# The order of VectorE's work around the start of a feed-forward: squares ahead of a low part, and a weight split behind a sum

## What is computed

```python
def second_block(x, mem, ...):
    for l in range(DEPTH):                       # DEPTH = 2
        ...
        y = memory_cross_attention(h, mem, xa_wq[l], xa_wkv[l], xa_wo[l], xa_mem_norm[l])
        x = x + rms_norm_2(y, g[3])
        h = rms_norm_2(x, g[4])
        y = sq_relu_mlp(h, mlp_w1[l], mlp_w2[l]) # jnp.square(relu(h @ w1)) @ w2, 1024 -> 4096 -> 1024
        x = x + rms_norm_2(y, g[5])
```

## Time and profile before

| | us |
|---|---|
| time, median of 3 runs (lowest, highest) | 1379.44 (1379.16, 1380.48) |
| the profiled execution | 1378.3 |
| its span, first to last instruction | 1376.5 |
| TensorE busy | 1361.0 (99%) |
| VectorE busy | 1013.3 (74%) |
| ScalarE busy | 743.4 (54%) |
| GpSimd busy | 98.0 (7%) |

### The profile page before, as it was taken

The page is one execution under the profiler, slowest core; times in us unless marked ns, Lnnn a source line. Parts: engine busy times, 40 slices in busy tenths (PEclk is TensorE's granted clock), DMA queues, the critical chain, the costliest instruction groups (busy, mean ns, idle before and its releaser), DMA issues.

```text
span 1376.5 us, 19424 instructions
## 1 busy us (share of the span) xinstructions
PE 1361.0 (99%) x7455; PEld 1135.9 (83%) x7455; DVE 1013.3 (74%) x1514; ACT 743.4 (54%) x1151; POOL 98.0 (7%) x104
## 2 busy tenths in 40 slices
PE   9999999999999999999999999999999999999998
PEld 6887888888888888888888778888888868888886
DVE  5666778777764777877787786886676876886665
ACT  4564555554545655654555666654445675654443
POOL 0000011000000000211111001120000000200000
PEclk9999999999999999999999999999999999999999
DMA  9844455555465435666655524368866523356552
GB/s 309 245 145 153 159 178 185 185 193 195 163 213 183 139 107 183 221 206 206 206 187 167 153 79 154 107 217 225 210 193 210 168 94 129 117 188 196 197 185 92
DMA packets 146578, 242.26 MB, mean 176 GB/s; under 512 B 4603, under 2 KB 91403, under 8 KB 146222
## 3 DMA queue, kind: packets, MB, share of 16 engines
q1 hardware_dynamic: 142498, 226.97, 50.5%
q0 software_dynamic: 3712, 13.77, 3.7%
q10 hardware_dynamic: 276, 0.27, 0.1%
HBM read 239.03 MB, written 1.97 MB: 175 GB/s over the span
## 4 chain that ended last, share of the span: by engine, by line
PE 92%; DVE 5%; ACT 2%; issue 1%; DMA 0%; POOL 0%; ACTq 0%; DVEq 0%
PE ps L1080 19%; PE ps L1046 16%; PE ps L1053 16%; PE ps L1050 16%; PE ps L1083 9%; PE ps L1186 3%; PE ps L1245 2%; PE ps L1260 2%; PE ps L1291 1%; DVE wlo L2490 1%; PE ps L1279 1%; PE ps L1856 1%; PE ps L1124 1%; PE ps L1122 1%; PE ps L1123 1%
## 5 line engine op out<-in xcount | busy, mean ns | idle before, releaser
L2490 DVE TENSOR_TENSOR wlo<-raw,whi 128x1024 fp32r<-128x1024 f32 (+2 forms) x427 | 532.7, 1259 | 192.4 <-ACT whi L1978 191.3
L1978 ACT CAST whi<-raw 128x1024 fp32r<-128x1024 f32 (+1 forms) x431 | 445.1, 1042 | 259.6 <-PE ps L1053 159.9
L1080 PE MATMUL ps<-act,whi 128*128 128x512 f32 x1152 | 315.8, 394 | 0.4 <-DVE act L2520 0.4
L1046 PE MATMUL ps<-whi,mhi 128*128 128x512 f32 (+2 forms) x688 | 236.8, 393 | 1.3 <-DVE mlo L2517 0.8
L1053 PE MATMUL ps<-whi,mlo 128*128 128x512 f32 (+2 forms) x688 | 231.4, 385 | 0.0
L1050 PE MATMUL ps<-wlo,mhi 128*128 128x512 f32 (+2 forms) x688 | 231.1, 385 | 0.0
L1080 PEld LDWEIGHTS ps<-act,whi 128*128 128x128 f32 x1152 | 199.3, 189 | 29.6 <-DVE act L2520 1.2
L1083 PEld LDWEIGHTS ps<-act,wlo 128*128 128x128 f32 x1152 | 177.6, 189 | 25.0
L1083 PE MATMUL ps<-act,wlo 128*128 128x256 f32 x1152 | 184.3, 281 | 0.0
L1053 PEld LDWEIGHTS ps<-whi,mlo 128*128 128x128 f32 x688 | 129.2, 188 | 26.6
L1050 PEld LDWEIGHTS ps<-wlo,mhi 128*128 128x128 f32 x688 | 129.4, 188 | 26.1 <-issue 0.2
(11 more groups left out here) (315 smaller groups left out, 1530.9 us busy)
## 6 DMA issues: line engine op xcount, KB each, us to landing
raw<-in_mlp_w SPq DMA_DIRECT2D x64, 1024.0 KB, 5.3
raw<-in_w_up SPq DMA_DIRECT2D x44, 1024.0 KB, 5.2
raw<-in_w_in SPq DMA_DIRECT2D x38, 1024.0 KB, 5.1
raw<-in_w_down SPq DMA_DIRECT2D x22, 1024.0 KB, 5.0
raw<-in_ev_w_in SPq DMA_DIRECT2D x10, 1024.0 KB, 5.1
raw<-in_w_out SPq DMA_DIRECT2D x8, 1024.0 KB, 5.0
raw<-in_xa_wkv SPq DMA_DIRECT2D x4, 1024.0 KB, 5.2
raw<-in_ev_w_out SPq DMA_DIRECT2D x4, 1024.0 KB, 5.2
```

Source lines behind the costliest of these rows:

```text
L1046: nc.tensor.matmul(o, hi[:, kx, rows_], wh[:, k, c0:c0 + w], start=first and h == 0 and k == 0 and (tt == 0 or at[1] == 0), stop=False)
L1080: nc.tensor.matmul(both, wh[:, k, w], act2[:, kx].rearrange("p i n -> p (i n)"), start=kx == 0, stop=False)
L1978: nc.scalar.copy(whi[:, m % HL, 0:w], raw[:, n % RAW, h * w:h * w + w]).then_inc(hi_done, 1)
L2490: nc.vector.tensor_tensor(wlo[:, m % HL, 0:w], raw[:, n % RAW, h * w:h * w + w], whi[:, m % HL, 0:w].bitcast(F32), ALU.subtract).then_inc( ...
```

## The change

In each layer of block two, on VectorE's queue alone: the squares of tile 0 (and the wait for x ahead of them) move from behind `up_lo(1, 3)` to before it; and in step b = 1 the low part of the second half of w2(0) (n0 + 21) is made directly behind the sum of the step, no longer behind its square. Nothing is added or taken away.

```diff
-                for g in range(4):
+                for g in range(3):
                     up_lo(1, g)
+                dve.wait_ge(x_ready, x_count("yx", l))
+                squares(("xm", l), lambda tt: x[:, tt, :], D, (0,))
+                up_lo(1, 3)
                 split_half(n0 + 17)
-                dve.wait_ge(x_ready, x_count("yx", l))
-                squares(("xm", l), lambda tt: x[:, tt, :], D)
+                squares(("xm", l), lambda tt: x[:, tt, :], D, (1,))
                 split_half(n0 + 18)
 
                 for b in range(NMB):
@@ -3393,7 +3395,7 @@
 
                     dve.wait_ge(m_low, g + 1)
                     nc.vector.tensor_tensor(two(up_a), halves_of(step_bank(b))[0], two(low_part), ALU.add).then_inc(m_sum, 1)
-                    if b == 0:
+                    if b <= 1:
                         split_half(2 * n + 5)
 
                     dve.wait_ge(row_ready, row_at("xm", l))
```

## The result

The changed kernel takes 1382.96 us (median of 9 runs, 1382.42 to 1383.38) against 1379.44 us (9 runs, 1378.57 to 1380.77): ratio 1.0026, 95% interval 1.0018 to 1.0034, 3.5 us slower. Forecast were 1383.2 us and +3.8 us.

A forecast was written before the change was run, and what follows sets the result against it. TensorE, 92% of the chain, was taken as the bound, so VectorE edits count only where TensorE stands still. 1.90 us in each of two layers gives +3.80 on 1379.44, 1383.2 us, range 1380.9 to 1384.3.

The forecast's parts named there:

- The hold: Tile 0's squares stand until GpSimd's second low part of w1(1) ends, taking 3.33 us and ending 1.09 us behind it.
- The stall at up_lo(1, 3): TensorE waits 1.37 us before high(0, 1, 3) for VectorE's up_lo(1, 3), now behind the squares; before, no wait.
- The transposes: TensorE reaches the transposes of the reciprocal root's row 1.16 us later: 1.37 us stall less the 0.21 us wait removed.
- up_b(0): VectorE's up_b(0), set by ScalarE's copy of the row, and all hanging on it down to sum(1), come 1.05 us later.
- The second edit: Low part w2(0) half 1 behind sum(1) removes TensorE's 0.25 us down-projection wait but delays up_b(1) by a further 0.94 us.
- The low part of w1(3) half 1: On VectorE it comes 1.99 us later (1.05 + 0.94); TensorE, with 0.09 us slack, stalls 0.99 us.
- half 0: Low part of w1(3) half 0 ready at 916.14, TensorE there at 916.23: no wait.
- The sum: TensorE loses 1.99 - 0.09 = 1.90 us in each of block two's two layers, +3.80 us in all.
- the squares first: Rival, chance 0.10: VectorE's squares get in before GpSimd's second low part; 0.95 us per layer, 1381.3 us.
- the late split: Rival, chance 0.09, said it does not bite: w1(3) half 1 in time; +0.91 us per layer, 1381.3 us.
- sharing: Rival, chance 0.05: squares beside GpSimd only stretched to 1.7 or 2.2 us; +0.53 us per layer, 1380.5 us.
- the best case: Rival, chance 0.02: both TensorE waits go, nothing new; -0.46 us per layer, 1378.5 us.

The follow-up runs named there:

- ScalarE's squares with the early cast: Kernel before, tile 0's squares moved to ScalarE, plus the second edit and ScalarE casting w1(3) half 0 ahead of mhi(1): 1377.41 us against 1379.44, ratio 0.9986.
- the early cast: Kernel before with the second edit alone, and ScalarE casting w1(3) half 0 ahead of mhi(1): 1378.47 us against 1379.40, ratio 0.9993.

## Why the prediction was right

**The hold.** Forecast 3.33 us for the squares of tile 0, measured 3.32 and 3.34. The runs in which GpSimd's second low part waits, and in which it is missing, show that the cause is GpSimd's instruction and nothing in VectorE's queue.

**The stall at up_lo(1, 3).** Forecast 1.37 us; by the spacing of the matmuls TensorE went on 902.30 - (900.58 + 0.48) = 1.24 us late. up_lo starts together with the short read-out, not behind it.

**The transposes.** Forecast +1.16 us, measured +0.98: a stall of 1.24 us instead of 1.37, matmuls right behind it that are 0.10 us slower in all, and a removed wait worth 0.37 us here instead of the 0.21 shown. 1.24 + 0.10 - 0.37 = 0.97.

**up_b(0).** Forecast +1.05 us, measured +0.79 (17.23 us behind the last matmul of the cross-attention's output, before 16.44): ScalarE's copy of the row moved by 0.92, and up_b(0) starts 0.41 us behind the copy's start, where before it started 0.54 us behind it, in VectorE's own queue. Of the 0.26 us missing, 0.18 are the transposes'; the copy starts 0.41 us behind them and not 0.47.

**The second edit.** From sum(1) to up_b(1) +0.94 forecast, +0.93 measured. The low part of w1(3) half 1, forecast +1.99, came +1.72 us later, all of the difference being up_b(0)'s. The forecast had half 0 just in time (0.09 us in hand). That was wrong: TensorE waited for it, 0.26 us as shown. TensorE was there 0.65 us earlier than forecast, since w2(0) came 0.86 us late and not 1.16, and since the wait taken away in w2(0) had cost about 0.60 us and not 0.25; the low part was only 0.27 us earlier. The error did not reach the sum, since half 1 sets what follows. Stall there: 0.99 us forecast; 0.73 shown as idle, 0.90 by the spacing (918.53 to 921.30 against 916.23 to 918.10).

**The sum.** 1.90 us per layer forecast, 1.73 and 1.75 measured. Two terms were off, and they partly cancel: up_b(0) made VectorE's chain 0.27 us less late, so w1(3) half 1 started +1.63 us instead of +1.90; and the matmuls behind that stall are 0.10 us slower (921.30 to 924.21 against 918.10 to 920.91), which the prediction did not count. 1.63 + 0.10 = 1.73. The rivals: the squares first was made to happen, by a semaphore, and costs 2.27 us in all (1.9 forecast); the late split bites by itself (1.90 us alone); sharing is excluded by the 3.3 us; the best case of -0.46 us per layer was too small, since both waits together are worth about 1.1 us per layer, as ScalarE's squares with the early cast show.

## What to carry to other kernels

An idle time ahead of an instruction can be filled only by work that the engine may start then: before an instruction is moved into it, look what the other engines have running in that very stretch, here a GpSimd instruction that also reads SBUF and that began about 0.15 us earlier. And a split that fills the time of a chain through another engine (square, cast, split) is free where it stands; moved ahead of the chain it lengthens it, unless the other engine's link is taken out of the chain first, as the early cast does. Where two small edits lengthen the same chain, their prices add, and each should be tried alone.

## What the runs showed of the hardware

A VectorE instruction with two SBUF operands that meets a running GpSimd instruction with SBUF operands ends 1.08 to 1.10 us behind GpSimd's end in every case looked at (1.22 us is its length alone), however much of it overlaps: 3.32, 3.13, 2.32 and 1.69 us long. up_lo, which reads PSUM and SBUF, keeps its 0.61 us beside GpSimd. ScalarE's cast of 128 x 1024 keeps its 1.05 us, beside GpSimd's low part (897.82 in the kernel before) and without it (887.58).

GpSimd stands for VectorE too. In the kernel before, the same root takes 0.70 us where VectorE does nothing (383.69) and 1.64 us in the earlier trace rows, where it starts during VectorE's low part and ends 0.58 us behind it. And in block one:

```profile
383.69 0.70 POOL L869 TENSOR_TENSOR rstd<-ss,small 128x2 f32<-128x2 f32 x1 [34.33 <-DVE ss L2543]
```

```profile
203.95 3.41 POOL L932 TENSOR_TENSOR work<-work 128x512 f32<-128x512 f32 x1 [5.55 <-DVE work L2849]
```

```profile
205.52 0.68 DVE L2891 TENSOR_TENSOR mlo<-work,mhi 128x512 fp32r<-128x512 f32 x1
206.12 2.32 DVE L2490 TENSOR_TENSOR wlo<-raw,whi 128x1024 fp32r<-128x1024 f32 x1
```

The same multiply takes 1.29 us in later steps (231.27). Here it starts, by its row, during an instruction of VectorE with two SBUF operands (203.79), and two more of VectorE that start later, at 204.38 and 205.52, run at full speed; GpSimd's ends at 207.36, and only the low part of 206.12 is held, to 1.08 us behind that. So the one that runs keeps the other out, but who asked first does not settle who is next: VectorE's back-to-back instructions passed a waiting GpSimd. The squares of this change met GpSimd's second low part about 0.15 us after its start, and no run here shows what a smaller distance would do.

The Trainium skill, SBUF — State Buffer, section Who interferes with whom, says that a VectorE instruction with two SBUF inputs contends with a GpSimd instruction that reads SBUF, that this is an exclusive lock, and that the order of issue decides who blocks. The traces agree on the lock: GpSimd's own two low parts stay at 2.4 us each while VectorE's squares take 3.32 or 3.13. On the order they agree for the squares and the root, and not, by the start in its row, for the multiply of 3.41 us. The Trainium skill, Perfetto Trace Analysis, section GPSIMD Engine Instruction, warns that a GpSimd span is unreliable. For the low parts that did not matter here: the row of 4.75 us for two told who came first, with about 0.15 us to spare. The row of 3.41 us, however, holds the waiting along with the work.

Unexpected was the price of a wait of TensorE: an idle time of 0.21 us in the profile cost 0.49 us by w2(0), one of 0.25 us cost 0.60 us.
